# Two-layer hybrid encoder on one core: the start of the down projection bank by bank, and six chunks instead of four summed by VectorE for the second LayerNorm's mean

## The chip, the cores and the metric

The kernel runs on one core of one Trainium2 chip. The metric is device time in microseconds (us) of one execution. The core has a TensorE for matrix products (PE; PEld is its weight load, and "weights" below are also the model's weights), a VectorE (DVE), a ScalarE (ACT), a GpSimd that hardly works here, and a SyncE queue (SP) that issues the DMAs. PSUM has eight banks of 128 x 512 fp32 each, here called bank0 to bank7.

## The reference

One inference step over 320 tokens (256 of a prompt, 64 of a sample) through two layers. In each layer three branches (latent attention, mLSTM, gated MLP) are merged, and then comes the part that matters here:

```
x = LN(alpha*x + mix);  x = LN(alpha*x + MoE(x))

def _swiglu(x, wg, wu, wd):
    return (jax.nn.silu(x @ wg) * (x @ wu)) @ wd

def _moe(...):
    ...
    out = _swiglu(xf, sg, su, sd)                    # the shared expert
    for e in range(N_EXPERTS):                       # 16, in 4 groups of 4
        out = out + gate[:, e:e + 1] * _swiglu(xf, wg[e], wu[e], wd[e])

def _layernorm(x, g, b):
    mu = jnp.mean(xf, -1, keepdims=True)
    var = jnp.mean(jnp.square(xf - mu), -1, keepdims=True)
    y = (xf - mu) * lax.rsqrt(var + EPS)
```

D_MODEL is 1024, the hidden width of an expert 256. All inputs are fp32. A token uses one group of four experts and two experts inside it.

## The kernel before

**Layout.** Activations are kept transposed: 8 chunks of 128 features (KD = 8) by 320 tokens (T). A matrix of weights comes in blocks of 128 x 1024 fp32, 512 KB each, 179 a layer (NB). Every block is loaded by SP into one of 8 raw buffers (`w32`, line 428), rounded to fp16 by ACT (`whi`, `hi_at`, line 549), and its rounding error is formed by DVE (`wlo`, `lo_at`, line 1042); `whi` and `wlo` have 4 slots each. ACT may write a slot when the block four places back has been used (`blk_done`), and SP may load a raw buffer when `lo_at` has read the block eight places back. Each product is three fp16 passes (hi*hi, hi*lo, lo*hi).

**The experts.** Tokens are gathered by group of experts, at most 128 a group. For each of the 16 experts e PE uses four blocks (line 1732, each 24 matmuls of 128 columns) and writes two banks: bank1 and bank2 for even e, bank3 and bank0 for odd e (`UPB = [1, 2, 3, 0]`). DVE forms the hidden tile in four steps: lines 1651, 1655, 1659 and, after ACT has rounded it (line 967), 1664. Line 1655 is the last that reads the two banks, and raises `e_free`; line 1664 raises `e_lo`. Between these steps DVE works through four blocks, `lo_e(1)` to `lo_e(4)`: three ahead of line 1651, one behind line 1659. All of this is written out by hand, so the program's text sets the order on every engine.

**The down stage.** The output is formed in two halves of four chunks. A half is one block for the shared expert (block D0 or D1; `down`, line 2170, 24 matmuls of 320 columns into four banks), then four groups of four blocks (`group_down`, line 2253, 24 matmuls of 512 columns a group), then a `scatter` (line 2269) that adds the groups' rows back to their tokens in the four banks. For the first half the shared block goes to bank0 to bank3, the same banks that the experts wrote: so PE waits on line 2276 until `e_free` has counted all 16 experts. `group_down` waits on line 2241 until `e_lo` has counted all 16. ACT and DVE split each group's result (lines 973 and 1672).

**The end of the layer.** `half_out` calls `residual` for chunk c as its bank is done: DVE adds the bank to `acc` (line 1087), and ACT squares it (line 578). LayerNorm needs the mean and the mean square over all 1024 features. `stats` does both on PE with a matrix of ones in fp32. `SUMMED` says up to which chunk DVE sums beforehand (line 1092), so that PE takes one matmul for that sum (line 1768) and one for each other chunk (line 1771). For the second LayerNorm (k = 1) it is 3: DVE sums chunks 0 to 3 after the first half, PE adds chunks 4 to 7. The squares are summed by DVE (`add_square`, line 1112); PE takes that sum on line 1779, and the last square by itself on line 1776. Then ACT squares the mean (line 555), and DVE centres and scales (lines 1051 to 1055).

The branch of the program behind `Else`, for more than 128 tokens in a group, isn't taken in these runs: the profile's rows are those of the `If` side.

Of the kernel before, what the change touches and what calls it, by code (L numbers as in the profile page):

```python
# [34 lines left out]
ALU = mybir.AluOpType  # L35
# [4 lines left out]
P = 128  # L40
DM, L = 1024, 2
TP, TS, PAST = 256, 64, 256
T = TP + TS
KD = DM // P
# [48 lines left out]
def slot(l, n):  # L93
    return (l * NB + n) % SLOTS
# [23 lines left out]
def build_trunk(nc, d):  # L118
    with ExitStack() as ctx:
# [259 lines left out]

        N_CONST = 13  # L380

        SUMMED = (KD - 2, 3)
        MEAN_BANK, SQ_BANK = 6, (5, 7)

        def out_bank(c):
# [649 lines left out]
        def _(dve):  # L1035
# [50 lines left out]
            def residual(l, k, c, b):  # L1086
                V.scalar_tensor_tensor(acc[:, c * T:(c + 1) * T], b[:, 0:T], UN,
                                       acc[:, c * T:(c + 1) * T], ALU.mult, ALU.add
                                       ).then_inc(y_done.sem, 1)
                if 0 < c <= SUMMED[k]:  # L1090
                    dve.drain()
                    a = V.tensor_tensor(var[:, 0, :], acc[:, 0:T] if c == 1 else var[:, 0, :],
                                        acc[:, c * T:(c + 1) * T], ALU.add)
                    if c == SUMMED[k]:
                        a.then_inc(y_sum.sem, 1)
                if k == 0 and c > 1:
                    add_square(l, k, c - 1)
                if k == 0 and c == KD - 1:
                    add_square(l, k, c)
                if k == 1 and c in (2, 3):  # L1100
                    add_square(l, k, c - 1)
                if k == 1 and c == 3:
                    add_square(l, k, c)
                if k == 1 and c == KD - 1:
                    for n in range(4, KD - 1):
                        add_square(l, k, n)

            def add_square(l, k, c):

                dve.wait_ge(y_sq.sem, y_sq.value(l, KD * k + c + 1))  # L1110
                dve.drain()
                V.tensor_tensor(var[:, 1, :], ysq[:, 0, :] if c == 1 else var[:, 1, :], ysq[:, c % 4, :],
                                ALU.add).then_inc(sq_sum.sem, 1)
# [10 lines left out]
            for l in range(0, L):  # L1124
# [501 lines left out]
                with dve.If(fits):  # L1626
                    shared_lo()

                    dve.wait_ge(g_hi.sem, g_hi.value(l, 1))
                    V.tensor_tensor(gate_lo[0:EXPERTS, :], bank[4][0:EXPERTS, :], gate_hi[0:EXPERTS, :],  # L1630
                                    ALU.subtract).then_inc(g_lo.sem, 1)
                    lo_lead(U0 + 4)
                    W2 = 2 * CAP

                    def two(ap):
                        return ap.rearrange("p (f n) -> p f n", f=2)

                    for ee in range(0, EXPERTS // 2):
                        for e2 in range(2):
                            e = ee * 2 + e2  # L1640
                            g0 = e * 4 + (U0 + 4)

                            def lo_e(j):
                                lo_at(l, g0 + (j + LEAD))

                            lo_e(1)
                            lo_e(2)
                            lo_e(3)

                            dve.wait_ge(e_tanh.sem, e_tanh.value(l, e + 1))  # L1650
                            V.scalar_tensor_tensor(h1[:, 0:W2], ht[:, 0:W2], 1.0,
                                                   bank[UPB[2 * e2]][:, 0:W2], ALU.add, ALU.mult)
                            dve.drain()  # L1653
                            dve.wait_ge(blk_done.sem, blk_done.value(l, g0 + 4))
                            V.tensor_tensor(h1[:, 0:W2], h1[:, 0:W2], bank[UPB[2 * e2 + 1]][:, 0:W2],
                                            ALU.mult).then_inc(e_free.sem, 1)
                            dve.drain()
                            dve.wait_ge(gb_ps.sem, gb_ps.value(l, e + 1))
                            V.tensor_tensor(two(h2[:, 0:W2]), two(h1[:, 0:W2]),
                                            bank[4 + 2 * e2][:, 0:CAP].unsqueeze(1).broadcast_to(  # L1660
                                                [P, 2, CAP]), ALU.mult).then_inc(e_prod.sem, 1)
                            lo_e(4)
                            dve.wait_ge(e_hi.sem, e_hi.value(l, e + 1))
                            V.scalar_tensor_tensor(hlo[:, bass.ds(e * W2 + H0, W2)], h2[:, 0:W2],
                                                   UN * UN * XS / (2 * GS),
                                                   hhi[:, bass.ds(e * W2 + H0, W2)], ALU.mult,
                                                   ALU.subtract).then_inc(e_lo.sem, 1)

                    def group_out(g, g2, hf):

                        dve.wait_ge(yg_hi.sem, yg_hi.value(l, g + (4 * hf + 1)))
                        V.scalar_tensor_tensor(y_lo[:, bass.ds(g * 512, 512)],
                                               bank[(4, 2)[hf] + g2][:, :], UN * XS,
                                               y_hi[:, bass.ds(g * 512, 512)], ALU.mult, ALU.subtract
                                               ).then_inc(yg_lo.sem, 1)

                    for gg in range(0, GROUPS // 2):
                        for g2 in range(2):
                            for j in range(4):
                                n = D0 + 4 + 4 * g2 + j  # L1680
                                lo_at(l, gg * 8 + n)
                            group_out(gg * 2 + g2, g2, 0)
                    half_out(0)
                    for g in range(GROUPS):
                        for j in range(4):
                            lo_lead(D1 + 3 + 4 * g + j - LEAD)
                        group_out(g, g % 2, 1)
                    for s_ in (u_free, u_prod, u_lo):
                        dve.sem_inc(s_.sem, 2 * EXPERTS)
                    half_out(1)  # L1690
                    ln_vector(l, 1, C_L2G, C_L2B, lambda: lo_lead(NB - 1))
                    lo_at(l, NB + LEAD)
# [30 lines left out]
        def _(pe):  # L1723
# [77 lines left out]
            for l in range(0, L):  # L1801
# [385 lines left out]
                with pe.If(fits):  # L2187
# [49 lines left out]
                    def group_down(g, g2, hf):  # L2237

                        b = bank[(4, 2)[hf] + g2]

                        pe.wait_ge(e_lo.sem, e_lo.value(l, EXPERTS))
                        pe.wait_ge(xg_ev.sem, xg_ev.value(l, 20))
                        pe.wait_ge(ot_ev.sem, ot_ev.value(l, GROUPS))
                        if hf:
# [28 lines left out]
                                a.then_inc(sums.sem, 1)  # L2273

                    pe.wait_ge(u_lo.sem, u_lo.value(l, 2))
                    pe.wait_ge(e_free.sem, e_free.value(l, EXPERTS))
                    down(l, D0, slot(l, D0), half0, 0, True, False)
                    for gg in range(0, GROUPS // 2):
                        for g2 in range(2):
                            group_down(gg * 2 + g2, g2, 0)  # L2280
# [201 lines left out]
```

## Time and profile before

| | before |
|---|---|
| median of 3 runs | 1082.61 us (1082.49, 1082.61, 1086.24) |
| the profiled execution | 1087.75 us |
| its span, first to last instruction | 1086.0 us |
| PE busy in the span | 1023.6 us (94%) |
| DVE busy | 827.3 us (76%) |
| ACT busy | 660.3 us (61%) |
| mean granted TensorE clock | 0.986 |
| read from HBM | 198.77 MB |

The profile is one execution seen by the hardware profiler. A busy time is the union of the instructions of an engine. A timeline row gives the start, the length and the instruction, in brackets the engine's idle time before it and what ended it. "issue" there stands for an end that the profile doesn't put down to anything. Matmuls are pipelined, so the length of one (0.30 us for 320 columns) is longer than the distance between two starts; times on PE are best read from start to start. The granted clock is 1.00 at 2.4 GHz and 0.50 at 1.2 GHz.

### The profile page before, as it was taken

What the parts mean: (1) busy time and instruction counts of PE and PEld (TensorE: products, weight loads), DVE (VectorE), ACT (ScalarE), POOL (GpSimd) and SP (SyncE); (2) the same over time, 40 slices, a digit from 0 to 9 for tenths busy, and PEclk for the clock granted to TensorE, in tenths of its full rate; (3) what the DMA queues carried; (4) which work ended last, traced back from release to release, by engine and by line L of the source; (5) the groups of instructions that cost most, each with busy time, mean ns of one, the idle gap of its engine ahead of it and who ended that gap; (6) DMA issues with size and microseconds to landing.
All of it is one profiled execution on the core that took longest, in us unless ns stands there. A gap on an engine that the chain in (4) does not pass through costs nothing. (4 is left out here: it accounts for less than half of the span.)

```text
span 1086.0 us, 24604 instructions
## 1 busy us (share of the span) xinstructions
PE 1023.6 (94%) x10126; PEld 786.3 (72%) x10126; DVE 827.3 (76%) x1484; ACT 660.3 (61%) x1059; POOL 0.7 (0%) x10
## 2 busy tenths in 40 slices
PE   6999999999998799999999999999999978999995
PEld 4877777777776699965567777777777658999443
DVE  4786677654898699989887766676559877999886
ACT  5565455754365777767767445556534676777764
POOL 0000000000000000000000000000000000000000
PEclk9999999999999899999999999999999998999998
DMA  9754444323462389988735534443244415999861
GB/s 348 268 167 143 140 142 129 108 98 116 156 235 78 114 299 327 333 281 312 280 118 192 165 122 137 141 139 98 98 136 156 155 45 187 332 324 328 294 260 51
DMA packets 59653, 205.06 MB, mean 189 GB/s; under 512 B 7088, under 2 KB 10348, under 8 KB 59020
## 3 DMA queue, kind: packets, MB, share of 16 engines
q1 hardware_dynamic: 55980, 195.96, 53.2%
q10 hardware_dynamic: 3552, 7.42, 1.9%
q8 instruction: 84, 1.38, 0.5%
q14 instruction: 37, 0.30, 0.1%
HBM read 198.77 MB, written 3.40 MB: 186 GB/s over the span
## 5 line engine op out<-in xcount | busy, mean ns | idle before, releaser
L1042 DVE SCALAR_TENSOR_TENSOR wlo<-w,whi 128x1024 f16<-128x1024 f32 x358 | 429.7, 1220 | 76.9 <-ACT whi L549 75.3
L549 ACT ACTIVATE whi<-w 128x1024 f16<-128x1024 f32 x358 | 370.6, 1049 | 93.6 <-PE bank L1732 52.2
L1732 PE MATMUL bank<-xhi,whi 128*128 128x320 f16 x704 | 211.0, 300 | 0.0
L1732 PE MATMUL bank<-xhi,wlo 128*128 128x320 f16 x704 | 210.5, 299 | 0.0
L1732 PE MATMUL bank<-xlo,whi 128*128 128x320 f16 x704 | 210.5, 299 | 0.0
L1732 PE MATMUL bank<-arena_b,whi 128*128 128x128 f16 x2048 | 183.4, 222 | 0.0
L1732 PE MATMUL bank<-arena_b,wlo 128*128 128x128 f16 x1024 | 179.2, 222 | 0.0
L1732 PEld LDWEIGHTS bank<-arena_b,whi 128*128 128x128 f16 x2048 | 160.0, 99 | 0.0
L1732 PEld LDWEIGHTS bank<-arena_b,wlo 128*128 128x128 f16 x1024 | 101.6, 99 | 0.0
L1732 PEld LDWEIGHTS bank<-xhi,whi 128*128 128x128 f16 x704 | 68.8, 98 | 30.3 <-issue 2.5
L1732 PEld LDWEIGHTS bank<-xhi,wlo 128*128 128x128 f16 x704 | 68.9, 98 | 26.8
L1732 PEld LDWEIGHTS bank<-xlo,whi 128*128 128x128 f16 x704 | 68.9, 98 | 26.1 <-issue 1.4
L1755 PE MATMUL bank<-whi,xhi 128*128 128x128 f16 (+1 forms) x384 | 66.4, 220 | 0.0
L1755 PE MATMUL bank<-wlo,xhi 128*128 128x128 f16 (+1 forms) x384 | 66.0, 219 | 0.0
L1755 PE MATMUL bank<-whi,xlo 128*128 128x128 f16 (+1 forms) x384 | 66.0, 219 | 0.0
L1732 PE MATMUL bank<-br_hi,whi 128*128 128x320 f16 x192 | 57.4, 299 | 0.0
L1732 PE MATMUL bank<-br_lo,whi 128*128 128x320 f16 x192 | 57.4, 299 | 0.0
L1732 PE MATMUL bank<-br_hi,wlo 128*128 128x320 f16 x192 | 57.4, 299 | 0.0
L2253 PE MATMUL bank<-whi,arena_a 128*128 128x512 f16 x128 | 48.6, 379 | 1.8 <-DVE wlo L1042 1.8
L2253 PE MATMUL bank<-wlo,arena_a 128*128 128x512 f16 x128 | 48.5, 379 | 0.0
L2253 PE MATMUL bank<-whi,arena_b 128*128 128x512 f16 x128 | 48.5, 379 | 0.0
L694 ACT ACTIVATE arena_a<-bank,par_h 128x320 f32<-128x320 f32 x24 | 12.7, 527 | 58.6 <-PE bank L1732 58.6
(357 smaller groups left out, 1751.6 us busy)
## 6 DMA issues: line engine op xcount, KB each, us to landing
w<-in_w SPq DMA_DIRECT2D x358, 512.0 KB, 4.7
arena_b<-head_rows ACTq DMA_DIRECT2D x2, 1920.0 KB, 7.2
xT<-in_x SPq DMA_DIRECT2D x2, 640.0 KB, 4.9
out_y<-xT SPq DMA_DIRECT2D x4, 320.0 KB
rows<-in_rows ACTq DMA_DIRECT2D x1, 1024.0 KB, 11.3
rows<-in_rows SPq DMA_DIRECT2D x1, 1024.0 KB, 5.8
out_ckv<-arena_a SPq DMA_DIRECT2D x2, 320.0 KB
acc<-kr SPq DMA_DIRECT2D x2, 288.0 KB
```

Of the source, the lines that this page charges most:

```text
L549: A(whi[:, n % SLOTS, :], w32[:, n % RAW, :], ACT.Copy, scale=WS).then_inc(hi_done.sem, 1)
L694: A(dst, bank[(M0 + step) % 4][:, 0:T], func, scale=scale, bias=par_t[:, bass.ds(col, 1)]).then_inc(z_ev.sem, 1)
L1042: V.scalar_tensor_tensor(wlo[:, n % SLOTS, :], w32[:, n % RAW, :], WS, whi[:, n % SLOTS, :], ALU.mult, ALU.subtract).then_inc(lo_done.sem, 1)
L1732: ins = M(out, w[:, s, sub * P:(sub + 1) * P], rhs(part, k), start=(n == 0), stop=(n == 3 * len(subs) - 1))
L1755: ins = M(bank[b][0:m, i * P:(i + 1) * P], x[:, k, t0:t0 + m], w[:, s, k * P:(k + 1) * P], start=(j == 0), stop=(j == 3 * KD - 1))
L2253: a = M(b[:, :], h_[:, bass.ds(g * (8 * CAP) + ((2 * q + kt) * CAP + H0), CAP)], w[:, slot(l, n), kt * 512:(kt + 1) * 512], start=(q == 0 ...
```

## The change

Four things are changed in the text of the program; no arithmetic is added but the two sums, and the matmuls of the down stage are the same ones.

1. The first half's shared block is written out bank by bank in the order of `UPB`: six matmuls for bank1, six for bank2, then bank3, then bank0. Ahead of bank1 PE waits for 15 experts in `e_free`, ahead of bank3 for the 16th. The second half's shared block still goes through `down`.
2. `group_down` of group g waits for 4(g + 1) experts in `e_lo`, not for 16.
3. For the last expert DVE does `lo_e(3)` behind line 1659 (now 1665), not ahead of line 1651 (now 1657).
4. `SUMMED` of the second LayerNorm is 5, not 3: DVE adds chunk 4 after the residual of chunk 5, chunk 5 after that of chunk 6, and the square of chunk 4 moves ahead of the residual of chunk 7. PE takes chunks 6 and 7.

```
-        SUMMED = (KD - 2, 3)
+        SUMMED = (KD - 2, KD - 3)
...
-                if 0 < c <= SUMMED[k]:
-                    dve.drain()
-                    a = V.tensor_tensor(var[:, 0, :], acc[:, 0:T] if c == 1 else var[:, 0, :],
-                                        acc[:, c * T:(c + 1) * T], ALU.add)
-                    if c == SUMMED[k]:
-                        a.then_inc(y_sum.sem, 1)
+                late = k == 1 and c > 3
+                if late and c > 4 or not late and c:
+                    n = c - 1 if late else c
+                    if n <= SUMMED[k]:
+                        dve.drain()
+                        a = V.tensor_tensor(var[:, 0, :], acc[:, 0:T] if n == 1 else var[:, 0, :],
+                                            acc[:, n * T:(n + 1) * T], ALU.add)
+                        if n == SUMMED[k]:
+                            a.then_inc(y_sum.sem, 1)
...
+                if k == 1 and c == KD - 2:
+                    add_square(l, k, 4)
                 if k == 1 and c == KD - 1:
-                    for n in range(4, KD - 1):
-                        add_square(l, k, n)
+                    add_square(l, k, 5)
+                    add_square(l, k, 6)
...
-                            lo_e(3)
+                            if e < EXPERTS - 1:
+                                lo_e(3)
...
+                            if e == EXPERTS - 1:
+                                lo_e(3)
                             lo_e(4)
...
-                        pe.wait_ge(e_lo.sem, e_lo.value(l, EXPERTS))
+                        pe.wait_ge(e_lo.sem, e_lo.value(l, 4 * (g + 1)))
...
-                    pe.wait_ge(e_free.sem, e_free.value(l, EXPERTS))
-                    down(l, D0, slot(l, D0), half0, 0, True, False)
+                    pe.wait_ge(e_free.sem, e_free.value(l, EXPERTS - 1))
+                    ready(l, D0)
+                    for b in UPB:
+                        if b == UPB[2]:
+                            pe.wait_ge(e_free.sem, e_free.value(l, EXPERTS))
+                        for kt in range(2):
+                            for w, h_ in ((whi, hhi), (whi, hlo), (wlo, hhi)):
+                                a = M(bank[b][:, 0:T], w[:, slot(l, D0), (4 * kt + b) * P:(4 * kt + b + 1) * P],
+                                      h_[:, kt * T:(kt + 1) * T], start=(kt == 0 and w is whi and h_ is hhi),
+                                      stop=False)
+                    a.then_inc(blk_done.sem, 1)
```

PE at the start of the down stage, before. A row is line, operation, tile written and tiles read (arena_a holds the hidden tile's high part, arena_b its low part and, at line 1732, the gathered tokens), size, and what it waits for:

```order
L1732 MATMUL bank0<-arena_b,wlo 128x128
L2170 MATMUL bank0<-arena_a,whi 128x320 [waits lo_done,e_free,u_lo]
L2170 MATMUL bank0<-arena_b,whi 128x320
L2170 MATMUL bank0<-arena_a,wlo 128x320
L2170 MATMUL bank1<-arena_a,whi 128x320
L2170 MATMUL bank1<-arena_b,whi 128x320
L2170 MATMUL bank1<-arena_a,wlo 128x320
L2170 MATMUL bank2<-arena_a,whi 128x320
```

The same place now, with the wait for the last expert in the middle:

```order
L2291 MATMUL bank2<-arena_a,whi 128x320
L2291 MATMUL bank2<-arena_b,whi 128x320
L2291 MATMUL bank2<-arena_a,wlo 128x320
L2291 MATMUL bank3<-arena_a,whi 128x320 [waits e_free]
L2291 MATMUL bank3<-arena_b,whi 128x320
L2291 MATMUL bank3<-arena_a,wlo 128x320
```

The twelve matmuls of bank1 and bank2 stand ahead of that wait; the first of them waits for 15 experts where all 24 waited for 16.

DVE at the last expert (the third row in each is line 1655, now 1661, which frees the banks), before:

```order
L1042 SCALAR_TENSOR_TENSOR wlo<-w32,whi 128x1024 [waits hi_done] x3
L1651 SCALAR_TENSOR_TENSOR mk<-mq,bank3 128x256 [waits e_tanh]
L1655 TENSOR_TENSOR mk<-mk,bank0 128x256 [waits blk_done]
L1659 TENSOR_TENSOR mo<-mk,bank6 128x256 [waits gb_ps]
L1042 SCALAR_TENSOR_TENSOR wlo<-w32,whi 128x1024 [waits hi_done]
L1664 SCALAR_TENSOR_TENSOR arena_b<-mo,arena_a 128x256 [waits e_hi]
```

And now:

```order
L1042 SCALAR_TENSOR_TENSOR wlo<-w32,whi 128x1024 [waits hi_done] x2
L1657 SCALAR_TENSOR_TENSOR mk<-mq,bank3 128x256 [waits e_tanh]
L1661 TENSOR_TENSOR mk<-mk,bank0 128x256 [waits blk_done]
L1665 TENSOR_TENSOR mo<-mk,bank6 128x256 [waits gb_ps]
L1042 SCALAR_TENSOR_TENSOR wlo<-w32,whi 128x1024 [waits hi_done] x2
L1672 SCALAR_TENSOR_TENSOR arena_b<-mo,arena_a 128x256 [waits e_hi]
```

One block's low part has moved from ahead of the three steps to behind them.

DVE at the end of the layer (mu_var holds the two sums), before:

```order
L1087 SCALAR_TENSOR_TENSOR acc<-bank4,acc 128x320 [waits sums,acc_pre]
L1087 SCALAR_TENSOR_TENSOR acc<-bank5,acc 128x320 [waits sums]
L1087 SCALAR_TENSOR_TENSOR acc<-bank0,acc 128x320 [waits sums]
L1087 SCALAR_TENSOR_TENSOR acc<-bank1,acc 128x320 [waits sums]
L1112 TENSOR_TENSOR mu_var<-mu_var,ysq 128x320 [waits y_sq] x3
```

And now:

```order
L1087 SCALAR_TENSOR_TENSOR acc<-bank4,acc 128x320 [waits sums,acc_pre]
L1087 SCALAR_TENSOR_TENSOR acc<-bank5,acc 128x320 [waits sums]
L1095 TENSOR_TENSOR mu_var<-mu_var,acc 128x320
L1087 SCALAR_TENSOR_TENSOR acc<-bank0,acc 128x320 [waits sums]
L1095 TENSOR_TENSOR mu_var<-mu_var,acc 128x320
L1117 TENSOR_TENSOR mu_var<-mu_var,ysq 128x320 [waits y_sq]
L1087 SCALAR_TENSOR_TENSOR acc<-bank1,acc 128x320 [waits sums]
L1117 TENSOR_TENSOR mu_var<-mu_var,ysq 128x320 [waits y_sq] x2
```

Two sums and one square now stand ahead of the residual of the last chunk (bank1).

## Rows read from the trace of the kernel before

**Rows 1.** The page's chain of work that ended last: shares by engine.
```profile
PE 34%; DVE 6%; ACT 3%; issue 1%; DVEq 1%; ACTq 0%
```
**Rows 2.** That chain in order of time (start, us, what), second layer.
```profile
1006.99 2.59 issue
1009.58 5.09 PE bank L2170 x24
```
**Rows 3.** Timeline of PE, first layer (start, us, line, idle before).
```profile
474.41 0.22 PE L1732 MATMUL bank<-arena_b,wlo 128*128 128x128 f16 x1
477.22 0.30 PE L2170 MATMUL bank<-arena_a,whi 128*128 128x320 f16 x1 [2.59 <-issue]
477.35 0.30 PE L2170 MATMUL bank<-arena_b,whi 128*128 128x320 f16 x1
...
482.15 0.38 PE L2253 MATMUL bank<-whi,arena_a 128*128 128x512 f16 x1
```
**Rows 4.** Timeline of DVE there, the last expert.
```profile
472.79 3.50 DVE L1042 SCALAR_TENSOR_TENSOR wlo<-w,whi 128x1024 f16<-128x1024 f32 x3
476.21 0.41 DVE L1651 SCALAR_TENSOR_TENSOR mk<-mq,bank 128x256 f32<-128x256 f32 x1
476.69 0.42 DVE L1655 TENSOR_TENSOR mk<-mk,bank 128x256 f32<-128x256 f32 x1
...
477.55 1.22 DVE L1042 SCALAR_TENSOR_TENSOR wlo<-w,whi 128x1024 f16<-128x1024 f32 x1
...
483.50 5.11 DVE L1042 SCALAR_TENSOR_TENSOR wlo<-w,whi 128x1024 f16<-128x1024 f32 x4 [4.39 <-ACT whi L549]
```
**Rows 5.** Timeline of ACT, same place.
```profile
482.41 1.06 ACT L549 ACTIVATE whi<-w 128x1024 f16<-128x1024 f32 x1 [4.33 <-PE bank L2170]
```
**Rows 6.** PE, second layer's second shared block: first matmul, first one behind it.
```profile
1040.13 0.30 PE L2170 MATMUL bank<-arena_a,whi 128*128 128x320 f16 x1
...
1043.39 0.38 PE L2253 MATMUL bank<-whi,arena_a 128*128 128x512 f16 x1
```
**Rows 7.** Stretches: length, busy PE PEld DVE ACT POOL, granted clock, DMA share, GB/s.
```profile
477.22:482.15 4.93, 4.93 (x25) 3.03 (x25) 1.88 (x3) 0.42 (x1) 0.00 (x0) 0.65 0.90 322
482.15:502.87 20.72, 20.72 (x99) 9.41 (x96) 19.16 (x18) 18.01 (x19) 0.00 (x0) 1.00 0.81 296
502.87:507.53 4.66, 4.51 (x33) 3.05 (x32) 3.87 (x8) 1.75 (x5) 0.00 (x0) 1.00 0.99 390
...
1009.58:1014.52 4.94, 4.94 (x25) 3.04 (x26) 1.88 (x3) 0.42 (x1) 0.00 (x0) 0.65 0.95 338
...
337.08:358.39 21.31, 20.47 (x225) 14.77 (x225) 16.50 (x53) 13.54 (x25) 0.00 (x0) 0.92 0.10 33
870.58:890.69 20.11, 19.09 (x225) 14.21 (x225) 16.51 (x53) 13.54 (x25) 0.00 (x0) 1.00 0.11 35
```
**Rows 8.** Timeline of PE, end of the first layer.
```profile
537.29 0.70 PE L1768 MATMUL bank<-mu_var,ones_dm 128*128 128x320 f32 x2
537.83 2.32 PE L1771 MATMUL bank<-acc,ones_dm 128*128 128x320 f32 x8
539.98 0.70 PE L1776 MATMUL bank<-ysq,ones_dm 128*128 128x320 f32 x2
```
**Rows 9.** Timeline of DVE, same place.
```profile
535.12 0.89 DVE L1087 SCALAR_TENSOR_TENSOR acc<-bank,acc 128x320 f32<-128x320 f32 x2 [0.66 <-PE bank L2269]
536.40 0.49 DVE L1087 SCALAR_TENSOR_TENSOR acc<-bank,acc 128x320 f32<-128x320 f32 x1 [0.39 <-PE bank L2269]
537.49 0.49 DVE L1087 SCALAR_TENSOR_TENSOR acc<-bank,acc 128x320 f32<-128x320 f32 x1 [0.59 <-PE bank L2269]
538.08 1.66 DVE L1112 TENSOR_TENSOR mu_var<-mu_var,ysq 128x320 f32<-128x320 f32 x3
540.65 0.89 DVE L1051 TENSOR_TENSOR acc<-acc,bank 128x320 f32<-128x320 f32 x2 [0.92 <-ACT mu_var L555]
```
**Rows 10.** Timeline of ACT, same place.
```profile
540.18 0.44 ACT L555 ACTIVATE mu_var<-bank 128x320 f32<-128x320 f32 x1 [1.70 <-PE bank L1771]
```

## The prediction, made before the changed kernel was run

> **What bounds the kernel now.** I read three views. The first is the chain of work that ended last: by engine PE has by far the largest share, and a part of it is "issue", idle PE time that the profile puts down to nobody [rows 1]. In order of time one such piece stands between the last expert's matmuls and the shared block of the down stage: 2.59 us, and the 24 matmuls behind it take 5.09 us [rows 2]. The second view is the timelines of the three engines there. The last expert matmul starts at 474.41, the first of the shared block at 477.22 [rows 3]. What ends the pause can be told from DVE: line 1655 of the last expert starts at 476.69 and takes 0.42, so it ends at 477.11 [rows 4], 0.11 before PE starts. That is the step that raises `e_free`, and PE waits for 16 of them. The block's own weights had been ready since about 474.0 (the first of three steps of 3.50 us that start at 472.79 [rows 4]). The third view is the table of stretches: the 24 matmuls take 4.93 and 4.94 us at a mean granted clock of 0.65 in the two layers [rows 7], while the same 24 in the second half take 1043.39 - 1040.13 = 3.26 us [rows 6]. So a pause of 2.8 us is followed in this execution by a stretch in which the clock was partly at the 1.2 GHz level, and that costs a further 4.93 - 3.26 = 1.67 us a layer.
>
> At the layer's end the chain goes through the mean: ACT's square of it starts at 540.18 [rows 10], straight after PE's ninth and tenth fp32 pass; DVE waits for that, 0.92 us idle [rows 9].
>
> **Part 1, the start of the down stage.** Start to start a 320-column matmul is 477.35 - 477.22 = 0.135 us [rows 3]. The new order lets PE go on one matmul behind 474.41; by its 128 columns that is some 0.06 (0.135 x 128 / 320), so at 474.47. Experts 0 to 14 freed their banks long before: DVE had started on the next three weight steps at 472.79, and line 1655 of expert 14 stands ahead of these [rows 4]. Twelve matmuls for bank1 and bank2 take 12 x 0.136 = 1.63 us, until 476.10.
>
> Meanwhile DVE does two weight steps instead of three. Three take 3.50 with 1.22 for the last, so two end 1.14 earlier [rows 4]. Line 1655 then ends at 477.11 - 1.14 = 475.97, 0.13 before PE asks for bank3. No wait is left, or at most 0.05. The other twelve end at 477.73, where the groups now start at 482.15 [rows 3]. With the clock at its upper level the old order would have come there at 477.22 + 3.26 = 480.48. **The pause is worth 480.48 - 477.73 = 2.75 us a layer, the clock behind it 1.67 more.**
>
> What is late next? The moved step (block D0 + 2) takes the place behind line 1659 that was D0 + 3's: it starts at 477.55 - 1.14 = 476.41 and ends at 477.63. PE wants it one block behind the groups' start, 477.73 + 1.30 = 479.03 (16 blocks in 20.72 us are 1.295 each [rows 7]): 1.4 us of cover, at no cost. The step behind it (D0 + 3) keeps its time, 477.55 to 478.77 [rows 4], and is wanted at 480.3. Behind the moved step on DVE's queue stands also line 1664, whose `e_lo` the fourth group alone now needs. SP's load of the raw buffer that the moved step frees is issued 1.3 us later; its data are wanted eight blocks on, so this is covered too. Block D0 + 4 starts when PE has used D0: ACT at 482.41 and DVE at 483.50 [rows 4, 5], 1.35 after the groups' start; now 479.08, when DVE has just finished line 1664 (478.69 and 0.42, as line 1655). It is wanted at 481.6 and done at 480.3. From there every engine follows PE as before.
>
> **The new wait of a group** (four of its own experts) is met either way: line 1664 of the last expert ends at about 479.1 and the first group needs only experts 0 to 3. With the old count of 16 the first group, due at 477.73, would have waited 1.4 us for it. So edit 2 is what keeps 1.4 of the 2.75; it isn't a gain of its own.
>
> **Loads.** The pause also gave the DMA time. From 477.22 to 502.87 it moved 322 x 4.93 + 296 x 20.72 = 7,720 KB in 25.65 us [rows 7], 301 GB/s. The same blocks must now come in 25.65 - 4.42 = 21.23 us, 364 GB/s. The scatter's stretch shows 390 [rows 7], and 0.81 of the engines' time in the long stretch says that the DMA had been waiting for free buffers. I cost it at nothing; the upper bound is a rival below.
>
> **Part 2, the mean.** Before, PE takes 10 fp32 passes from 537.29; the four chunks' eight passes start at 537.83 and the next thing at 539.98 [rows 8]: 0.54 a chunk. The last chunk's pair starts at 539.44. Now DVE: residuals 4 and 5 end at 536.01 [rows 9]. A drained step of this size starts 0.585 after the one ahead ((1.66 - 0.49) / 2 [rows 9]), an undrained one 0.40 (0.89 - 0.49). So: sum of chunk 4 at 536.10; residual 6 at 536.50 (was 536.40); sum of chunk 5 at 537.08 to 537.57, which raises `y_sum`; square 4 at 537.66; residual 7 at 538.06 to 538.55, which was 537.49. PE waits for `y_sum` and starts at about 537.70, 0.4 later than before; then chunk 6 at 538.24 and chunk 7 at 538.78, for which residual 7 is in time. Against 539.44 that is **0.67 us earlier a layer**. Squares 5 and 6 end at 539.7, the last matmul of `stats` is due at 539.9: covered by 0.1 to 0.2. The bounds: 1.08 (two chunks' passes, if DVE cost nothing) and -0.36 (if no part of the three added steps fell into DVE's pauses of 0.39 and 0.59 us [rows 9]: 3 x 0.585 = 1.75 later, residual 7 from 539.24 to 539.73 and chunk 7 at 539.80). I take 0.67, as each duration has a row.
>
> Here a rule speaks against the change. The rows show 0.40 between two undrained DVE steps of 0.49 us [rows 9]. The Trainium skill (VectorE: DVE Perf Modes, "The DRAIN you can't avoid") says that each DVE step is followed by a flush of about its duration less 266 ns before the next starts. By that, as an estimate from that page, steps of 0.49 would lie 0.71 apart, residual 7 would end at 539.6 and part 2 would lose 0.2 us a layer. The trace doesn't agree.
>
> **The sum.** Against the profiled execution: 2 x (2.75 + 1.67 + 0.67) = 10.2 us off 1087.75, 1077.6. But that execution is 5.14 above the median of 1082.61. Its trace has slow-clock stretches that can explain it: twice 1.67 here, and 21.31 against 20.11 us for the same work at 337 in the first layer and at 870 in the second, at clocks of 0.92 and 1.00 [rows 7], 1.20 more; together 4.5 of the 5.1. The highest of the three runs is 3.6 above the median, near 2 x 1.67. So I take it that the median run didn't have the fall of the clock behind the pause, and only the pause counts: 2 x (2.75 + 0.67) = 6.8. **1082.6 - 6.8 = 1075.8 us.** The Trainium skill (TensorE: Matmul & The Clock Gate, "What's actually happening") says that where the gate's transitions fall differs from run to run; three times alone can't show that.
>
> **Rivals.**
>
> *The clock's share comes too* (22%): the median run did have both falls, and the 5.1 is the profiler's or other stretches'. For it: both layers of the one trace show the fall at the same place. Then 2 x 5.09 off: 1072.4.
>
> *The added DVE steps all land on the path* (6%): residual 7 becomes the last arrival at the mean, 0.36 a layer lost by the lower bound above. 2 x (2.75 - 0.36) = 4.8 off, 1077.8. The 0.40 between undrained steps [rows 9] speaks against it. The drain rule of the Trainium skill's VectorE: DVE Perf Modes points this way.
>
> *The weights follow too late* (9%). DVE is busy 19.16 of 20.72 us in the first half's groups, and ACT 18.01 [rows 7], so neither can catch up. The cover of D0 + 4 is 1.3 us. If the chain blk_done, ACT, DVE slips by more, PE pauses inside the first group instead. Pricing that at half of the 2.75: 1082.6 - 2 x (1.37 + 0.67) = 1078.5.
>
> *The pause isn't what it seems* (5%). The profile calls it "issue", not DVE. If PE's sequencer were busy with something that the profile doesn't show, only part 2 and perhaps nothing else would come: 1082.6 - 1.3 = 1081.3. Against it: the 0.11 us between DVE's end and PE's start.
>
> *The DMA becomes the bound of the down stage, and it comes out slower* (3%). The deciding rate is 301 GB/s over these 25.65 us: above it there is a gain, at it none, below it a loss. At 270 GB/s the 7,720 KB take 28.6 us, 2.9 more; with part 2 that is 2 x (2.9 - 0.67) = 4.5 us slower, 1087.1. Against it: 390 GB/s in the next stretch.
>
> **How the numbers follow.** 55% for the forecast, 1075.8 with about 1 us to each side. The range takes in the clock's share below and the late weights above: 1071.8 to 1079.3. A measurement of this kernel can tell about 0.5% from no change, here 5.4 us, so the line is 1077.2. Below it lie the forecast (some of its width not) and the first rival: 0.78. Between: the drains, the late weights, the pause not understood and the rest: 0.19. Slower: 0.03.
>
> **What the profile afterwards would show.** PE's pause ahead of the shared block gone (under 0.2 us), in both layers, and the 24 matmuls in 3.26 us at clock 1.00; the groups' first matmul some 4.4 us earlier after the last expert's; the groups still 20.7 us. If instead the matmul of bank3 or of the third or fourth block in the first group stands behind an idle time, the second step is wrong. At the end: six fp32 passes for the mean, 0.3 to 0.4 us of idle PE ahead of them, and ACT's square of the mean 0.6 to 0.7 us sooner after the scatter. Wrong would be a gain under 4 us with the pause gone: then time came back elsewhere, in the groups or in new falls of the clock at other pauses.

## The result, and the profile of the changed kernel

| | before | changed |
|---|---|---|
| median | 1084.76 us (16 runs, 1079.04 to 1087.73) | 1076.45 us (16 runs, 1072.65 to 1081.96) |
| ratio | | 0.9937, 95% interval 0.9919 to 0.9955 |
| profiled execution | 1087.75 us | 1076.37 us |
| its span | 1086.0 us | 1074.6 us |

The change makes the kernel 0.63% faster, 6.8 us by the ratio, with 4.9 to 8.8 in its interval. The medians differ by 8.3 us, the means (1083.8 and 1076.9) by 6.9. Both kernels scatter by more than the change is worth (8.7 and 9.3 us from lowest to highest), so single runs tell little. Much of the scatter goes with the clock: in the 16 runs of the changed kernel the mean granted clock lies between 0.985 and 0.993, and a run is about 1 us slower for each 0.001 that it is lower. The three runs before the prediction had a median of 1082.61; with 16 it was 1084.76.

The start of the down stage, changed kernel, first layer. Timeline of PE (start, us, line; an idle time ahead would stand in brackets), the first two, the thirteenth and the last of the 24 matmuls:

```profile
470.92 0.30 PE L2291 MATMUL bank<-arena_a,whi 128*128 128x320 f16 x1
471.06 0.30 PE L2291 MATMUL bank<-arena_b,whi 128*128 128x320 f16 x1
...
472.55 0.30 PE L2291 MATMUL bank<-arena_a,whi 128*128 128x320 f16 x1
...
474.05 0.30 PE L2291 MATMUL bank<-arena_a,wlo 128*128 128x320 f16 x1
```

Against [rows 3]: no idle time ahead of the first matmul, and none ahead of the thirteenth (472.55), which is bank3's. And the timeline of DVE there, against [rows 4]:

```profile
469.25 2.36 DVE L1042 SCALAR_TENSOR_TENSOR wlo<-w,whi 128x1024 f16<-128x1024 f32 x2
471.53 0.41 DVE L1657 SCALAR_TENSOR_TENSOR mk<-mq,bank 128x256 f32<-128x256 f32 x1
472.02 0.42 DVE L1661 TENSOR_TENSOR mk<-mk,bank 128x256 f32<-128x256 f32 x1
472.53 0.42 DVE L1665 TENSOR_TENSOR mo<-mk,bank 128x256 f32<-128x256 f32 x1
472.87 2.35 DVE L1042 SCALAR_TENSOR_TENSOR wlo<-w,whi 128x1024 f16<-128x1024 f32 x2
475.14 0.42 DVE L1672 SCALAR_TENSOR_TENSOR arena_b<-mo,arena_a 128x256 f16<-128x256 f32 x1
475.53 5.11 DVE L1042 SCALAR_TENSOR_TENSOR wlo<-w,whi 128x1024 f16<-128x1024 f32 x4
```

Line 1661 ends at 472.44, 0.11 before bank3's first matmul. DVE has no pause left: where it had been idle for 4.39 us [rows 4], it goes straight from line 1672 to the groups' weights. The stretches (length, busy PE PEld DVE ACT POOL, granted clock, DMA share, GB/s), against [rows 7]:

```profile
470.92:474.18 3.26, 3.26 (x27) 2.32 (x25) 3.09 (x6) 2.31 (x4) 0.00 (x0) 1.00 0.97 327
474.18:494.90 20.72, 20.72 (x98) 9.41 (x96) 20.51 (x20) 18.01 (x19) 0.00 (x0) 1.00 0.99 373
1000.46:1003.73 3.27, 3.27 (x29) 2.32 (x26) 3.10 (x6) 2.31 (x4) 0.00 (x0) 1.00 1.00 348
336.60:356.70 20.10, 19.09 (x225) 14.21 (x225) 16.49 (x53) 13.54 (x25) 0.00 (x0) 1.00 0.11 34
```

The shared block takes 3.26 us at clock 1.00 instead of 4.93 at 0.65, in both layers. The groups take the same 20.72 us, but at a DMA share of 0.99 and 373 GB/s, where it was 0.81 and 296. And the stretch in the first layer that had run at clock 0.92 (21.31 us at 337) is at 1.00 here, in 20.10. The change doesn't touch it: the clock fell there in one execution and not in the other. It also goes the other way. Behind a pause of 2.4 us at 595 (587 now) the same matmuls, which the change doesn't touch either, run at 1.00 in the profile of the kernel before and at 0.72 in this one. Before, then now:

```profile
595.46:599.98 4.52, 4.52 (x33) 3.23 (x33) 3.89 (x13) 3.59 (x7) 0.00 (x0) 1.00 0.85 276
587.14:593.33 6.19, 6.19 (x34) 3.89 (x34) 4.46 (x13) 3.59 (x7) 0.00 (x0) 0.72 0.73 235
```

The end of the layer, second layer, DVE and then ACT (DVE's first row is the residuals of chunks 4 and 5):

```profile
1056.94 0.89 DVE L1087 SCALAR_TENSOR_TENSOR acc<-bank,acc 128x320 f32<-128x320 f32 x2 [0.66 <-PE bank L2277]
1057.92 0.49 DVE L1095 TENSOR_TENSOR mu_var<-mu_var,acc 128x320 f32<-128x320 f32 x1
1058.33 0.48 DVE L1087 SCALAR_TENSOR_TENSOR acc<-bank,acc 128x320 f32<-128x320 f32 x1
1058.91 0.49 DVE L1095 TENSOR_TENSOR mu_var<-mu_var,acc 128x320 f32<-128x320 f32 x1
1059.49 0.49 DVE L1117 TENSOR_TENSOR mu_var<-mu_var,ysq 128x320 f32<-128x320 f32 x1
1059.90 0.48 DVE L1087 SCALAR_TENSOR_TENSOR acc<-bank,acc 128x320 f32<-128x320 f32 x1
```

```profile
1061.37 0.44 ACT L555 ACTIVATE mu_var<-bank 128x320 f32<-128x320 f32 x1 [0.48 <-PE bank L1779]
```

ACT's square of the mean starts 4.43 us after the residual of chunk 4; before it was 540.18 - 535.12 = 5.06 [rows 9, 10]. That is 0.63 saved, 0.67 forecast. The first layer saves less:

```profile
529.12 0.49 DVE L1095 TENSOR_TENSOR mu_var<-mu_var,acc 128x320 f32<-128x320 f32 x1
530.06 0.49 DVE L1117 TENSOR_TENSOR mu_var<-mu_var,ysq 128x320 f32<-128x320 f32 x1 [0.45 <-issue]
```

DVE is idle for 0.45 us ahead of the square of chunk 4, with nothing named. With it the mean is there after 531.85 - 527.16 = 4.69 us, 0.37 saved.

### The profile page after: what moved, and what is told of

The parts are those of the page before. It is cut to its first block and busy times, and to the rows that moved or that the text cites. A ratio compares the mean times of both kernels' runs of the same rounds, so it can differ in the third digit from the quotient of the medians.

```text
span 1074.6 us, 24596 instructions
## 1 busy us (share of the span) xinstructions
PE 1018.0 (95%) x10118; PEld 780.6 (73%) x10118; DVE 828.8 (77%) x1488; ACT 660.6 (61%) x1059; POOL 0.7 (0%) x10
## 5 line engine op out<-in xcount | busy, mean ns | idle before, releaser
L1740 PE MATMUL bank<-arena_b,whi 128*128 128x128 f16 x2048 | 181.0, 220 | 0.0
L1740 PE MATMUL bank<-arena_b,wlo 128*128 128x128 f16 x1024 | 176.8, 220 | 0.0
```

Of the source, the lines that this page charges most:

```text
L1740: ins = M(out, w[:, s, sub * P:(sub + 1) * P], rhs(part, k), start=(n == 0), stop=(n == 3 * len(subs) - 1))
```

## The experiments

### The start alone

Edits 1 to 3 on the kernel before; `SUMMED` and the end of the layer as they were.

```
-        SUMMED = (KD - 2, KD - 3)
+        SUMMED = (KD - 2, 3)
```

> The start of the down stage alone (edits 1 to 3; DVE sums four chunks and PE takes four, as before). My theory: the PE pause ahead of the shared block is gone in both layers, worth 2 x 2.75 = 5.5 us, plus what the clock cost behind the pause in those executions in which it fell (up to 2 x 1.67). So 5.5 to 7 us off the median of before, and it carries four fifths of the whole change. Rival (the pause is a matter of PE's sequencer, not of VectorE's step): an idle time of over 1 us stays ahead of the shared block and the gain is under 2 us. Rival (the weights follow too late): the pause is gone but the 16 blocks of the groups take more than their 20.7 us.

Measured: 1075.75 us (6 runs) against 1082.93, ratio 0.9929 (0.991 to 0.9948), 7.7 us by the ratio, with 5.6 to 9.7 in its interval, where 5.5 to 7 were expected. From the last expert matmul's start to the first group's it is 3.32 us in both layers, as in the changed kernel (3.31), where it was 482.15 - 474.41 = 7.74 [rows 3]. The pause is gone, the groups keep 20.7 us, and this part carries the change: its interval can't be told from that of all four edits. Neither rival holds.

### The end alone

Edit 4 on the kernel before.

```
-        SUMMED = (KD - 2, 3)
+        SUMMED = (KD - 2, KD - 3)
```

> The end of the layer alone (edit 4: VectorE sums six chunks, PE takes two; the start of the down stage as before). My theory: ScalarE's square of the mean starts 0.67 us sooner after the residual of chunk 4 (5.06 us before), 1.3 us in all, too little for the timing to tell from none; the profile tells it. The changed kernel showed 4.69 us in the first layer, where VectorE sat idle 0.45 us ahead of the square of chunk 4 with nothing named, and 4.43 in the second. If that idle time belongs to the code's place, it should not stand at the same instruction here; if it belongs to the order of the steps, it should. Rival (the added steps all land on the path): 0.36 a layer lost, the residual of chunk 7 as last arrival.

Measured: 1081.21 us (12 runs), ratio 0.9981 (0.9961 to 1.0001), so 2.1 us with none inside the interval. The profile is clearer than the timing: 533.82 - 529.12 = 4.70 us in the first layer and 1065.23 - 1060.80 = 4.43 in the second, the same as in the changed kernel. The pause of 2.59 us ahead of the shared block is in both layers of this kernel, untouched. And in neither layer did the clock fall behind it; the 24 matmuls of the shared block in the two layers:

```profile
472.88:476.14 3.26, 3.26 (x25) 2.35 (x25) 1.88 (x3) 0.42 (x1) 0.00 (x0) 1.00 0.97 339
1004.33:1007.59 3.26, 3.26 (x25) 2.34 (x26) 1.95 (x3) 0.42 (x1) 0.00 (x0) 1.00 0.91 330
```

This is the pause of [rows 3] with the same matmuls behind it, in 3.26 us at 1.00 where the kernel before showed 4.93 at 0.65. So one profile with the pause has both falls, the other has none.

The idle 0.45 us stands at the same instruction in the first layer, which by the expectation spoke for the order of the steps. But up to there both kernels' code for DVE is equally long, so the run doesn't tell the two apart; the one with the writes, below, does.

### The clock by itself

The kernel before with 19 matmuls in PE's pause that nobody reads.

```
-                    pe.wait_ge(e_free.sem, e_free.value(l, EXPERTS))
+                    pe.wait_ge(e_free.sem, e_free.value(l, EXPERTS - 1))
+                    unread(UPB[0], 19)
+                    pe.wait_ge(e_free.sem, e_free.value(l, EXPERTS))
                     down(l, D0, slot(l, D0), half0, 0, True, False)
```

> The kernel before, with 19 matmuls that nobody reads put into PE's pause ahead of the shared block (into bank1, after 15 experts; 19 x 0.135 = 2.57 us, so the pause keeps its length and the shared block starts where it did). It measures the clock's share by itself. My theory: the 24 matmuls of the shared block take 3.26 us at clock 1.00 in both layers, and the median falls by what the clock cost in the mean execution: 0 if the typical execution before had no fall, 3.3 us if all had both. From 16 runs each (8.3 us between the medians, 6.8 by the ratio, against 6.8 without any clock share) I expect 0 to 2 us. Rival (the clock's share comes in full): 3.3 us faster, 1081.4.

Timeline of PE, then the stretches of the 24 matmuls in the two layers:

```profile
470.30 2.74 PE L1763 MATMUL bank<-exp_sel,mats 128*128 128x320 f16 x19
```

```profile
473.00:476.27 3.27, 3.27 (x25) 2.36 (x25) 1.89 (x3) 0.42 (x1) 0.00 (x0) 1.00 0.93 332
1003.55:1006.80 3.25, 3.25 (x25) 2.36 (x25) 1.89 (x3) 0.42 (x1) 0.00 (x0) 1.00 0.87 325
```

The shared block starts 2.76 us after the last expert (2.81 before) and takes 3.27 and 3.25 us at clock 1.00. Time: 1082.09 us (12 runs), ratio 0.999 (0.9974 to 1.0007). So the fall of the clock behind the pause is worth about 1.1 us in the mean execution, between a loss of 0.8 and a gain of 2.8. Its full price of 3.3 us in every execution is outside. It is what one profiled execution had shown, not what the typical one pays; the profile of the end alone, with the pause and without a fall, says the same.

### All sixteen experts for every group

The changed kernel with edit 2 undone.

```
-                        pe.wait_ge(e_lo.sem, e_lo.value(l, 4 * (g + 1)))
+                        pe.wait_ge(e_lo.sem, e_lo.value(l, EXPERTS))
```

> The changed kernel, but each group of the first half waits for all 16 experts again. My theory: the first group's first matmul waits for VectorE's last step of the last expert, 1.4 us of idle PE between the shared block and the group in each layer, 2.8 us slower than the changed kernel, so some 4 us faster than before. Rival (the wait had been met anyway, so edit 2 does nothing): the same time as the changed kernel, no idle time there.

Timeline of PE, first matmul of the first group, both layers:

```profile
475.64 0.39 PE L2261 MATMUL bank<-whi,arena_a 128*128 128x512 f16 x1 [1.27 <-DVE arena_b L1672]
...
1004.11 0.39 PE L2261 MATMUL bank<-whi,arena_a 128*128 128x512 f16 x1 [1.27 <-DVE arena_b L1672]
```

From the last expert's matmul to the group it is 4.75 us against 3.31: 1.44 a layer, and the row names the step that it waits for. 1078.29 us (6 runs), ratio 0.995 (0.9933 to 0.9968). Edit 2 looks as if it did nothing, since the wait had been met in the kernel before; once the block ahead of it is early, it decides over about half of the 2.75 us. That is the profile's answer; by time the ratio can't be told from the changed kernel's 0.9937.

### The low part back in its old place

The changed kernel with edit 3 undone.

```
-                            if e < EXPERTS - 1:
-                                lo_e(3)
+                            lo_e(3)
...
-                            if e == EXPERTS - 1:
-                                lo_e(3)
```

> The changed kernel with the block's low part back ahead of the last expert's three steps (edit 3 undone). My theory, from the record: the step that frees the last two banks ends 1.14 us later, PE needs 1.63 us for bank1 and bank2 and then waits about 1.1 us ahead of bank3, in both layers; 2.2 us slower than the changed kernel. Rival (PE asks for bank3 late enough anyway): no idle time, same time as the changed kernel.

Timeline of PE, bank3's first matmul, in both layers (line 1660 there is 1655 of the kernel before):

```profile
474.11 0.31 PE L2288 MATMUL bank<-arena_a,whi 128*128 128x320 f16 x1 [0.90 <-DVE mk L1660]
```

```profile
1004.37 0.31 PE L2288 MATMUL bank<-arena_a,whi 128*128 128x320 f16 x1 [0.90 <-DVE mk L1660]
```

4.39 us instead of 3.31, so 1.08 a layer where 1.1 was expected. 1078.42 us (10 runs), ratio 0.9946 (0.9927 to 0.9965), beside 0.9938 for the changed kernel on the same chip: the 2.2 us can't be told by time, as the intervals overlap. The rival is out by the row: PE does wait ahead of bank3. This profile also says what the pause before was: what had been called "issue" [rows 2, 3], at a matmul with three waits, is here, where `e_free` is waited for alone, put down to DVE's step on `mk`, the one that raises it. That step ends at 474.05, 0.06 us before PE goes on; before it was 0.11.

### The cover at the start, used up

Four drained copies on DVE behind the last expert's third step.

```
                             if e == EXPERTS - 1:
+                                for n in range(4):
+                                    dve.drain()
+                                    V.tensor_copy(h1[:, :], ht[:, :])
                                 lo_e(3)
```

> The changed kernel with four drained copies (128x320) put on VectorE behind the last expert's third step, ahead of the moved low part: 4 x 0.585 = 2.3 us more on VectorE there, in each layer. It tests the cover that the record gives: block D0 + 2 had 1.4 us, D0 + 4 had 1.3. Theory: PE waits 2.3 - 1.4 = 0.9 us ahead of the first group's second block, another 0.1 or so ahead of its fourth, and from there the groups keep their 5.18 us: 1.0 us a layer between the shared block and the scatter, not 2.3. Rival (ScalarE and VectorE have no room to catch up, so each microsecond on VectorE there is one on the path): 2.3 us a layer. Rival (there was no cover): idle time also ahead of the first block.

DVE in this kernel, the copies first, and then the four weights of the first group:

```profile
473.23 1.53 DVE L1671 COPY mk<-mq 128x320 f32<-128x320 f32 x4
474.68 2.35 DVE L1042 SCALAR_TENSOR_TENSOR wlo<-w,whi 128x1024 f16<-128x1024 f32 x2
476.95 0.42 DVE L1675 SCALAR_TENSOR_TENSOR arena_b<-mo,arena_a 128x256 f16<-128x256 f32 x1
477.28 4.62 DVE L1042 SCALAR_TENSOR_TENSOR wlo<-w,whi 128x1024 f16<-128x1024 f32 x4
```

A copy is shorter than the adds that I had priced it by: it takes 0.33 us, and each starts 0.40 us behind the one ahead. Counted from the last expert's matmul the low parts start 1.6 us later than in the changed kernel, not 2.3. The first block of the first group takes 1.57 us to the next instead of 1.29: 0.28 lost, and the record's cover of 1.4 gives 1.6 - 1.4 = 0.2. So far it holds. But the last stretch doesn't. PE waits again at the end, in the scatter:

```profile
497.98 2.89 PE L2280 MATMUL bank<-arena_a,arena_b 128*128 128x320 f16 x20 [0.79 <-DVE arena_b L1683]
```

In the changed kernel that wait is 0.38 us in the second layer and isn't listed in the first. From the last expert's matmul to the start of the last matmul of the second half's groups it is 54.84 and 54.86 us against 53.89 and 54.14 in the changed kernel: 0.95 and 0.72 lost of 1.6. In the first layer DVE gets back about 0.65 us on the way. It had stood still a little between its steps: the first group's four take 4.62 us here and 5.11 in the changed kernel, each later group's 4.62 and 4.66. The rest comes out where the scatter waits for DVE. So neither sum holds for 1.6 us: the theory gives 0.2 a layer, the rival "no room to catch up" 1.6. There is some room, most of it in the first group, and the theory had left the scatter out. The rival "there was no cover" is out, as nothing waits ahead of the first block. The run's time, one execution, is 1075.94 us beside 1086.82 for one of the kernel before; it can't tell a microsecond.

### What the idle 0.45 us belongs to

The changed kernel with eight one-element writes ahead of the second half's residuals, first layer alone.

```
+                    if l == 0:
+                        for n in range(8):
+                            V.memset(h1[0:1, n:n + 1], 0.0)
                     half_out(1)
```

> The changed kernel with eight one-element writes on VectorE ahead of the second half's residuals in the first layer alone, where VectorE had been idle 0.66 us (they change no result). If VectorE's 0.45 us of idle time (the square of chunk 4, first layer) belongs to the place of the code, it moves to another instruction, some eight earlier in the order of steps, or vanishes from there; then the mean's square starts 4.4 us after the residual of chunk 4, as in the second layer, not 4.69. Rival (it belongs to the steps' order and ScalarE's table load ahead of the squares in that layer): it stays at the same instruction with the same 0.45 us.

First layer, DVE:

```profile
527.35 0.17 DVE L1700 MEMSET mk<- 1x1 f32 x8
528.43 0.89 DVE L1087 SCALAR_TENSOR_TENSOR acc<-bank,acc 128x320 f32<-128x320 f32 x2 [0.91 <-PE bank L2280]
529.41 0.49 DVE L1095 TENSOR_TENSOR mu_var<-mu_var,acc 128x320 f32<-128x320 f32 x1
529.81 0.48 DVE L1087 SCALAR_TENSOR_TENSOR acc<-bank,acc 128x320 f32<-128x320 f32 x1
530.39 0.49 DVE L1095 TENSOR_TENSOR mu_var<-mu_var,acc 128x320 f32<-128x320 f32 x1
530.98 0.49 DVE L1117 TENSOR_TENSOR mu_var<-mu_var,ysq 128x320 f32<-128x320 f32 x1
```

The idle time is gone from line 1117, and the mean comes 4.43 us after the residual, as in the second layer. The order of the steps and ACT's table load are unchanged, so that rival falls: the gap belongs to the place in the code. Nothing is won, though. The first residual now comes later, 2.75 us after the start of the groups' last matmul (525.68) against 2.40 in the changed kernel. The kernel with the copies, whose code is longer by other instructions, has the same 2.75 in its first layer. The time of the one execution was 1076.79 us.

The traces say where the gap goes. Counted over all that DVE recorded, with its waits and drains, it stands ahead of the 960th instruction. In the changed kernel and the four others with edit 4 and nothing added ahead on DVE, that is the square of chunk 4. With the writes or the copies it is the first residual, which starts 0.41 us after the end of the wait ahead of it, where it is 0.05 otherwise. In the kernel before the 960th is a drain; it shows 0.14 us instead of 0.5, so the gap was there and cost nothing. Another stands 256 instructions earlier in every trace, at the same step of the program:

```profile
358.52 0.21 DVE L1574 TENSOR_TENSOR rt<-rt 128x48 f32<-128x48 f32 x1 [0.43 <-issue]
```

What happens at these counts was not tried.

### A version that is faster than both

In the changed kernel three groups of the second half begin their third block 0.30 us late by the row, 0.47 by the distance of starts:

```profile
511.06 0.39 PE L2261 MATMUL bank<-whi,arena_a 128*128 128x512 f16 x1 [0.30 <-DVE wlo L1042]
516.72 0.39 PE L2261 MATMUL bank<-whi,arena_a 128*128 128x512 f16 x1 [0.30 <-DVE wlo L1042]
522.38 0.39 PE L2261 MATMUL bank<-whi,arena_a 128*128 128x512 f16 x1 [0.30 <-DVE wlo L1042]
```

ACT waits for a group's result ahead of the weights that PE needs two blocks on. This kernel prepares the second half's weights one block further ahead, as the first half's are:

```
+                    hi_at(l, D1 + 3)
                     for c in range(4):
                         square(l, 1, c)
...
-                            hi_lead(D1 + 3 + 4 * g + j - LEAD)
+                            if g < GROUPS - 1 or j < 3:
+                                hi_at(l, D1 + 4 + 4 * g + j)
...
+                    lo_at(l, D1 + 3)
                     half_out(0)
...
-                            lo_lead(D1 + 3 + 4 * g + j - LEAD)
+                            if g < GROUPS - 1 or j < 3:
+                                lo_at(l, D1 + 4 + 4 * g + j)
```

> The changed kernel, with the second half's weights prepared one block further ahead, as the first half's are: ScalarE and VectorE do block D1 + 3 ahead of the first half's residuals, and then each group's four blocks one further on, so that the two blocks that now stand behind a group's result stand ahead of it in part. In the changed kernel three of the four groups of the second half start their last two blocks 0.48 us late (chain: 5.66 us from group to group against 5.18 in the first half). Theory: those waits go, 3 x 0.48 = 1.4 us a layer, 2.9 in all, 1073.6 against 1076.5. Rival (VectorE's added step ahead of the residuals delays the second shared block by as much): under 1 us. The profile tells both: group to group in the second half, and the idle time ahead of the second shared block.

Measured: 1071.46 us (6 runs), ratio to the kernel before 0.9888 (0.9863 to 0.9913). The chain in order of time shows all four groups in one piece:

```profile
1026.06 3.26 PE bank L2182 x24
1029.32 20.72 PE bank L2265 x96
```

It is 5.18 us from group to group now, so 3 x 0.47 = 1.4 us a layer, as expected; the second shared block starts no later. The medians differ by 4.7 us (1076.13 for the changed kernel on the same chip), more than the 2.9 that the profile explains. Most of the rest goes with the clock. The mean granted clock of the six runs is 0.9913 on average and that of the seven 0.9890; at about 1 us for each 0.001, that makes about 2 us, as an estimate. The profiled executions differ the same way: the clock fell at 337 and behind the pause at 590 in the changed kernel's and at neither in this one's. Whether the new order has any part in the higher clock, six runs don't show.

### The changed kernel once more

No edit.

> The changed kernel once more, beside the others on the same chip, as their measure: 0.63% faster than before, within 0.2%. Its profile also shows once more whether VectorE's idle 0.45 us ahead of the square of chunk 4 stands in the first layer alone.

1076.13 us (7 runs), ratio 0.9938 (0.9915 to 0.9961). The idle 0.45 us stands in the first layer alone again (4.70 and 4.43 us). And the stretch that ran in 20.10 us at clock 1.00 in the first profile of this same kernel takes 21.31 at 0.92 here:

```profile
336.29:357.60 21.31, 20.47 (x225) 14.76 (x225) 16.48 (x53) 13.54 (x25) 0.00 (x0) 0.92 0.10 33
```

## Why the prediction was right, point by point

**The pause is DVE's `e_free`.** Right. With edit 3 undone the profile itself names the step. The rival "the pause isn't what it seems" is out.

**2.75 us a layer from the pause.** Right: the distance from the last expert to the first group is 3.31 where the sum had 477.73 - 474.41 = 3.32. The parts were also as told: 1.08 for edit 3 (1.14 was DVE's step), 1.44 for edit 2 (1.4).

**1.67 us more from the clock, but not in the median.** Right that it doesn't come in full. Of the two profiled executions with the pause and nothing in it, one has both falls, 3.3 us, and the other none; in the mean they are worth about 1.1 (-0.8 to 2.8). I had put that at zero, and zero isn't excluded. The way I got there was weaker than it looked: the 5.1 us between the profiled run and the median of three came from three runs. With 16, the median is 1084.76 and the difference 3.0. The forecast of the changed kernel's time, 1075.8, is 0.65 from the measured one in part because two errors offset each other: a median of before that was 2.1 us low, and a clock share of about 1.1 left out. That closeness is luck; the gain by the ratio, 6.8 beside 6.8, is the fairer test, and its interval is 4 us wide.

**0.67 us a layer from the mean.** 0.63 in the second layer; 0.37 in the first, because of the gap ahead of DVE's 960th instruction, which a drain had hidden before. The bound of -0.36 (all added steps on the path) is out, and with it that rival: the undrained steps are 0.41 apart (1058.33 to 1057.92), as read from [rows 9]. The sentence on the flush that the prediction took from the Trainium skill (VectorE: DVE Perf Modes, "The DRAIN you can't avoid") doesn't describe these steps. The same paragraph says that a next step which isn't held starts earlier; I had left that out, and so made the rival look stronger than the page does.

**The weights follow in time.** Right for every block: no group's matmul waited in the first half. The reason was incomplete. I read 1.3 and 1.4 us of cover at the first blocks; the run with copies showed that DVE, busy for 20.5 of 20.7 us, gets back only 0.65 to 0.9 us of the 1.6. Most of the rest comes out at the scatter, so of 1.6 us only that much was free over the whole stage.

**The loads.** Costed at nothing, and PE waited for none. The sum for it was wrong and its result right by luck. It took 4.42 us off the stretch from 477.22 on, but 2.75 of them lie ahead of that point. From the last expert's matmul to the scatter it is 28.46 us before and 24.03 now:

```profile
474.41:502.87 28.46, 25.87 (x125) 12.51 (x122) 23.69 (x25) 20.36 (x23) 0.00 (x0) 0.94 0.84 307
470.87:494.90 24.03, 24.03 (x124) 11.77 (x122) 23.65 (x25) 20.37 (x23) 0.00 (x0) 1.00 0.98 366
```

307 GB/s over 28.46 us are 8,740 KB, and in 24.03 us that is 364 again; measured were 366. In the groups' stretch the DMA's share went from 0.81 to 0.99, which I hadn't said. That is less of a change than it looks: before, the last 16.9 us of that stretch (from 486.00) already ran at 0.96 and 355 GB/s, and only its start was slack. The rate that the DMA could reach at most no run here tests.

**The profiled sum.** 10.2 us off 1087.75 was worked out; the profiled execution fell by 11.4. The closeness is in part luck. From the last expert to the first group it is 7.74 - 3.32 = 4.42 a layer, 8.8; from the mean 1.0. The other 1.6 are a balance of places that the change doesn't touch: 1.2 less at 337, 1.6 less at 360 (22.09 against 20.53 us, clock 0.85 against 0.92) and 0.5 less at the very start, against 1.7 more at 587.

## What to carry to other kernels

When a wait counts "all of them", look at which buffers the waiting work touches first and order it so that the last ones come last; then move every other count that stood behind it, since a wait that had always been met becomes the next one to decide. Before pricing a fall of the clock by one profiled execution, fill the pause with idle matmuls and time that: it gives the share in the mean. When an engine is nearly busy throughout, look for the cover of a step at every place further down where that engine is waited for, and not at the next consumer alone: here the block behind the step lost 0.28 us and the scatter much of the rest.

## What the runs showed of the hardware

The clock falls behind a pause in some executions and not in others. The same pause of 2.8 us was followed by the same 24 matmuls in 4.93 and 4.94 us (clock 0.65) in the profile of the kernel before and in 3.26 us (1.00) in that of the end alone; filling the pause was worth 1.1 us (-0.8 to 2.8), not 3.3. Two profiled executions of one and the same kernel, the changed one, differ too: 20.10 us at 1.00 in one, 21.31 at 0.92 in the other. The Trainium skill (TensorE: Matmul & The Clock Gate, "What's actually happening") says that the place of the transitions varies from run to run, and these runs agree.

DVE has gaps of about 0.4 us, with nothing named, ahead of its 704th and 960th recorded instruction. The second stays at its count when instructions are put ahead, so that another step gets it. A drained fp32 copy of 128x320 takes 0.33 us and the next starts 0.40 us after it, where a drained add of the same size takes 0.49 and the next starts after 0.585.

The DMA kept 373 GB/s over 20.7 us at a share of 0.99, with no wait of PE for it.
